# Three expert columns of a retrieval layer gathered early, without the rows of eight partitions, and those rows gathered apart

## The reference

```
def peer(h, w_query, sub_keys, expert_down, expert_up):
    # 8 heads, K = 16 experts a head: 128 experts for each of 256 tokens
    ...
    cand_id = top_i[:, :, 0, :, None] * N_KEYS + top_i[:, :, 1, None, :]
    best_s, best_c = lax.top_k(cand_s.reshape(T, PEER_HEADS, K * K), K)
    expert_id = take_along_axis(cand_id..., best_c)      # T x 128 numbers
    gate = softmax(best_s)
    ...
    u = expert_down[ib]                                  # 128 rows of 1024 for each token
    a = einsum('pd,ped->pe', xb, u)
    act = gelu(a) * gb
    v = expert_up[ib]                                    # 128 more rows of 1024
    y = einsum('pe,ped->pd', act, v)
```

## Time and profile before

| | |
|---|---|
| median of 3 runs | 1139.67 us (1138.53 to 1140.38) |
| the profiled execution | 1139.47 us, its span 1137.6 us |
| busy: PE, DVE, ACT, POOL | 1023.0, 850.4, 420.2, 288.6 us |
| DMA queue q0 (the gathers) | 37152 packets, 268.45 MB |
| mean granted TensorE clock | 0.974 |

### The profile page before, as it was taken

How to read it: one execution, slowest core, us unless ns; L and a number is a source line. 1 busy time by engine, 2 the same in 40 slices (tenths; PEclk the granted TensorE clock), 3 DMA queues, 4 the chain that set the end, 5 groups by cost and what they waited for, 6 DMA issues and landing times.

```text
span 1137.6 us, 14403 instructions
## 1 busy us (share of the span) xinstructions
PE 1023.0 (90%) x5146; PEld 711.7 (63%) x5146; DVE 850.4 (75%) x1789; ACT 420.2 (37%) x839; POOL 288.6 (25%) x262
## 2 busy tenths in 40 slices
PE   7999999999999999999999998878777778787896
PEld 7999999999998877966665554333323233333342
DVE  6988699999867984676787775776776677677555
ACT  5646544444356654352332231221221122122121
POOL 0000000000000000144455544444434435344530
PEclk9999999999999999999999999999989989898999
DMA  9533479989828334599999999999999999999995
GB/s 357 222 139 103 149 253 356 335 302 329 307 81 329 134 112 168 215 366 422 421 420 422 420 421 421 421 421 421 422 422 421 422 420 422 422 421 422 420 423 206
DMA packets 68183, 378.61 MB, mean 333 GB/s; under 512 B 7568, under 2 KB 7952, under 8 KB 35600
## 3 DMA queue, kind: packets, MB, share of 16 engines
q0 software_dynamic: 37152, 268.45, 56.9%
q1 hardware_dynamic: 29808, 106.09, 25.5%
q10 hardware_dynamic: 1152, 3.15, 0.8%
HBM read 376.61 MB, written 1.05 MB: 332 GB/s over the span
## 4 chain that ended last, share of the span: by engine, by line
PE 42%; DMA 32%; DVE 18%; ACT 4%; issue 3%; POOL 0%; SPq 0%; DVEq 0%; ACTq 0%; POOLq 0%
DMA ring_sb<-in_peer,idsb 30%; PE pb L940 8%; PE pb L943 7%; DVE ring_lo L1483 5%; PE pb L437 5%; PE pb L440 5%; PE pb L465 3%; PE pb L894 3%; DVE ring_sb L2178 2%; DVE arena L1746 2%; PE pb L819 1%; PE pb L880 1%; PE pb L655 1%; ACT whi L1003 1%; DMA arena<-in_peer,idsb 1%
## 5 line engine op out<-in xcount | busy, mean ns | idle before, releaser
L940 PE MATMUL pb<-ring_sb,arena 128*128 128x512 f32 x276 | 157.7, 655 | 79.4 <-ACT arena L1417 79.4
L2178 DVE CUSTOM_DVE_ANT_0 ring_sb<-ring_sb,arena 128x1024 f32<-128x1024 f32 x138 | 168.7, 1224 | 74.1 <-DMA ring_sb<-in_peer,idsb 72.9
L2279 POOL DMA_INDIRECT ring_sb<-in_peer,idsb x136 | 149.9, 1102 | 230.2 <-PE pb L943 205.0
L437 PE MATMUL pb<-xhi,whi 128*128 128x256 f32 x704 | 178.8, 289 | 3.6 <-DVE arena L1912 2.0
L2279 POOL DMA_INDIRECT arena<-in_peer,idsb x38 | 46.2, 1217 | 525.8 <-DVE idsb L2069 475.4
L1412 ACT ACTIVATE arena<-arena 128x4 f32<-128x4 f32 (+2 forms) x77 | 15.7, 205 | 434.0 <-DVE arena L2178 434.0
L440 PE MATMUL pb<-xlo,whi 128*128 128x256 f32 x704 | 175.7, 285 | 0.2
L1483 DVE TENSOR_TENSOR ring_lo<-ring_sb,whi 128x1024 fp32r<-128x1024 f32 x126 | 147.6, 1218 | 11.7 <-ACT whi L1003 11.7
L943 PE MATMUL pb<-ring_sb,arena 128*128 128x512 f32 x276 | 153.2, 638 | 0.0
L940 PEld LDWEIGHTS pb<-ring_sb,arena 128*128 128x128 f32 x276 | 53.4, 205 | 155.9 <-issue 155.0
L437 PEld LDWEIGHTS pb<-xhi,whi 128*128 128x128 f32 x704 | 134.6, 191 | 7.5 <-issue 3.9
(11 more groups left out here) (393 smaller groups left out, 1765.0 us busy)
## 6 DMA issues: line engine op xcount, KB each, us to landing
ring_sb<-in_ada SPq DMA_DIRECT2D x48, 512.0 KB, 5.6
ring_sb<-in_w_gu SPq DMA_DIRECT2D x44, 512.0 KB, 6.8
ring_sb<-in_w_in SPq DMA_DIRECT2D x38, 512.0 KB, 8.0
ring_sb<-in_w_down SPq DMA_DIRECT2D x22, 512.0 KB, 6.0
ring_sb<-in_w_out SPq DMA_DIRECT2D x16, 512.0 KB, 3.5
ring_sb<-in_w_q SPq DMA_DIRECT2D x8, 512.0 KB, 4.0
whi_rows<-in_w_q SPq DMA_DIRECT2D x6, 512.0 KB, 8.2
ring_sb<-in_peer,idsb POOLq DMA_INDIRECT x136, 26.8
```

Of the source, the lines that this page charges most:

```text
L437: e.matmul(o, hi_w(u)[:, c], xh(k), start=start, stop=False, skip_group_check=skip)
L940: mm = e.matmul(pb[4 + 2 * tile][:, :], dgr[col % 8], o[:, 1024:1536], start=begin, stop=end)
L2178: e.tensor_tensor_reduce(o, o, h2t[tile], 1.0, 0.0, MUL, ADD, aa[:, col:col + 1]).then_inc(*VD.up(("dot", col)))
L2279: e.indirect_dma_start(rows_at[s], None, peer, bass.IndirectOffsetOnAxis(ap=idsb[:, col:col + 1], axis=0)).then_inc(s_row[s], 16)
```

## The change

Three columns, 237 to 239, are taken out of their place in POOL's sequence. They are issued between column 219 and column 220, from a copy of the expert numbers (`kept`) in which the partitions 28 to 31 and 60 to 63 hold a number past the end of the table: DVE adds the constant `away` (16384 on these eight partitions, 0 elsewhere). The gathers have a bounds check that skips such rows. Meanwhile SP copies the real numbers of these partitions (two blocks of 4 x 3) to `apart`, on partitions 0 to 3. Right after column 233 POOL waits for these copies and for each of the three early gathers, and issues two gathers of four rows for each of the three columns, into partitions 28 to 31 and 60 to 63 of its slot. A column's semaphore now reaches its value only after all three of its gathers. The three slots aren't given back to `free`. DVE, ACT and PE work through the columns in the old order.

```diff
+    put("away", NEXP * ((p // 4 == 7) | (p // 4 == 15)))
...
+        kept, apart = sb("kept", 4, U32), sb("apart", 8, U32)
...
+        APART = range(237, 240)
+        APART_AT = (28, 60)
...
                 e.dma_start(slot(u), src).then_inc(s_slot[place[u]], 16)
+            e.wait_ge(*VTI.at(14))
+            for i, p in enumerate(APART_AT):
+                e.dma_start(apart[0:4, 4 * i:4 * i + 3], idsb[p:p + 4, APART.start:APART.stop]).then_inc(s_apart, 16)
             e.wait_ge(s_out, 64)
...
+                if n == 14:
+                    e.wait_ge(*VTI.at(n))
+                    e.tensor_scalar(kept[:, 0:3], idsb[:, APART.start:APART.stop], c_("away"), None, ADD).then_inc(*VTI.up("kept"))
...
-            for col in range(256):
+            for col in [*range(220), *APART, *range(220, 237), *range(240, 256)]:
                 s, until = free.pop(0)
-                uses[s] += 1
+                uses[s] += 3 if col in APART else 1
...
+                if col in APART:
+                    i = col - APART.start
+                    if i == 0:
+                        e.wait_ge(*VTI.at("kept"))
+                    e.indirect_dma_start(rows_at[s], None, peer, bass.IndirectOffsetOnAxis(ap=kept[:, i:i + 1], axis=0),
+                                         bounds_check=NEXP - 1, oob_is_err=False).then_inc(s_row[s], 16)
+                    continue
...
+                if col == 233:
+                    e.wait_ge(s_apart, 32)
+                    for i, c in enumerate(APART):
+                        r, v = row_of[c]
+                        e.wait_ge(s_row[r], v - 32)
+                        for j, p in enumerate(APART_AT):
+                            e.indirect_dma_start(rows_at[r][p:p + 4], None, peer,
+                                                 bass.IndirectOffsetOnAxis(ap=apart[0:4, 4 * j + i:4 * j + i + 1], axis=0)).then_inc(s_row[r], 16)
```

More of the change, by code:

```diff
@@ L41 @@
 _at = 0
-for _name, _n in (("ones", 128), ("invf", 1), ("eps", 1), ("eps2", 1), ("one", 1), ("zero", 1), ("iota", 16), ("ident", 128),
+for _name, _n in (("ones", 128), ("invf", 1), ("eps", 1), ("eps2", 1), ("one", 1), ("zero", 1), ("iota", 16), ("away", 1), ("ident", 128),
                   ("rot", 128), ("bd64", 128), ("tri", 128), ("sbm", 128), ("hgm", 128), ("fold", 32)):
@@ L205, in build @@
         s_row = [sem(f"s_row{i}") for i in range(16)]
+        s_apart = sem("s_apart")
         s_up = [sem(f"s_up{i}") for i in range(2)]
```

## The result

The changed kernel takes **1143.66 us** (median of 6 runs, 1142.78 to 1144.51), the kernel before 1139.68 (6 runs, 1138.48 to 1140.38). The ratio is 1.0037, with a 95% interval of 1.0027 to 1.0048: **slower by 0.37%, 4.0 us**, where 1133.7 was forecast. The profiled execution took 1143.42 us with a span of 1141.6, also 4.0 longer than before.

The account below looks back on a forecast made before the run. The prediction took one late DMA engine as the bound: gathers ending at 1124.1 instead of 1130.0 give -5.9 us, all other terms 0, so 1133.7 us. Its own range was 1132.3 to 1135.5; the 8-in-10 range 1131.9 to 1140.5.

Parts of the forecast that it names:

- the load of one late engine: End of the gathers: fifteen DMA engines end by 1123.6 us, one at 1130.0, 6.4 us behind, and every column waits for it.
- its windows: Sign at the end: no lone engine at 0.06 beyond a microsecond or two; share falls to 0 around 1120 to 1124.
- The waits: POOL's waits for `kept`, the early landings and SP's two copies, before column 234 at the latest: 0 us added.
- POOL's six issues: Six four-row gathers behind column 233 take POOL 7.4 us; the queue keeps 12 us of margin, so cost 0.
- the dot of column 220: Behind the three early columns, columns 220 to 236 come some 1 to 2 us later; 237 to 239 give it back.
- column 233: On POOL, column 233 takes the place of the old 236 and goes out at 1055.17 us.
- if these eight are one engine's share, and the late engine's: Eight rows skipped in three early gathers: the late engine has 7.4 us less to do and ends at 1122.6.
- The chance of 0.66: Weight of the forecast, resting on the relieved engine being the late one.
- They return by six gathers of four rows ... I take 0.5 us, the even spread: Return of 24 rows over sixteen engines: 0.5 us taken, bounds 0 to 7.4; fifteen engines then end by 1124.1.
- The first: Rival: relief misses the late engine or comes back to it, which still ends last; 1140.0 us, chance 0.17.
- The third: Rival: the queue runs dry behind column 233 while POOL issues six gathers and waits; 1144 us, chance 0.08.
- The second: Rival: relief is real, but the 24 returned rows pile up on one of the fifteen; 1138 us, chance 0.09.

Follow-up runs that it names:

- e9: Kernel before, order unchanged, columns 237 to 239 gathered without the rows of partitions 12 to 15 and 44 to 47, never brought back: 1132.95 us against 1139.04.
- e2: Kernel before with columns 237 to 239 issued early but gathered whole, no four-row gathers or SP copies: 1138.76 us against 1139.15.
- e3: Changed kernel without the six four-row gathers and SP's copies, the skipped rows of 28/60 left out for good: 1138.89 us against 1139.15.
- e6: Kernel before, order unchanged, sixteen columns each gathered without the eight rows of a different partition set: 1136.92 us against 1139.3.
- e12: Kernel before plus six four-row gathers after column 236 into unused arena, four to 28/60, two to 92/124: 1142.96 us, ratio 1.0034.
- e14: e12 with all row numbers past the end of the table, so no data moves: 1138.97 us against 1139.14.
- e5: e3 with POOL held before column 234 until PE has used column 226: 1139.53 us against 1139.3.
- e13: e12 with each gather's four rows placed eight partitions apart: 1141.55 us, ratio 1.0020.
- e18: e12 with four gathers (16 rows), all to partitions 12 to 15 and 44 to 47: 1144.59 us, ratio 1.0049.
- e15: Kernel before plus six gathers of sixteen rows after column 236, on partitions 16 to 31, 64 to 79 and 80 to 95: 1146.85 us, ratio 1.0067.
- e17: e12 with four gathers (16 rows), all to partitions 28 to 31 and 60 to 63: 1142.43 us against 1138.98.
- e10: Changed kernel with partitions 12 to 15 and 44 to 47 in place of 28/60, nothing left out: 1140.29 us, ratio 1.0012.
- e16: Changed kernel at 12/44, one four-row gather after each of columns 228 to 233, nothing left out: 1139.42 us, ratio 1.0003.

## Why the prediction was wrong

**What held.** The bound is the load of one late engine: e9 gained 6.1 us where 5.9 to 6.4 was worked out, and its windows look as the prediction drew them. The waits cost nothing as costed: the move and `kept` by e2 and e3, SP's copies by what is left over (the whole change +4.0, the six gathers alone +3.9). POOL's six issues took 7.7 us, for 7.4. In before's kernel and this one alike one engine ends last, alone. Two times on the way were off and cost nothing: the dot of column 220 comes 7.3 us later than in before (1050.23 against 1042.94), not 1 to 2, and column 233 goes out at 1064.60, not at 1055.17; `e2` has the same gap and loses nothing.

**First step that failed: "if these eight are one engine's share, and the late engine's".** The first half held (e6, e9: one set of eight rows is one engine's, 2.5 us). The second did not: 24 rows off 28/60 saved 0.0 (e3). The chance of 0.66 rested on "by judgement and without a row", and the text itself said that fifteen of sixteen are others. The Trainium skill (DMA: Bandwidth & Descriptors, section The descriptor swizzle) gives 12/44 to engine 3, 28/60 to engine 7 and 92/124 to engine 15, and its section Latency and other measured facts calls 7 and 15 the usually slower ones. The runs agree on the set of 12/44 as one engine's share, but skipping the rows that the page gives to 7 or 15 gained nothing, and those of 3 gained 6.1 us; the measurement decides. What made the engine late here, q14's packets, the prediction didn't look for.

**Second step that failed: "They return by six gathers of four rows ... I take 0.5 us, the even spread".** It cost 3.9 us (e12). The upper bound written there, 7.4, held; the value was taken from the nearest rows, all of which show 128-row gathers. And it was added to the wrong place: as load on fifteen engines that had 6.4 us to spare. The late engine lost it too, +2.8 us at column 231 and +1.05 at column 234.

What the runs show of this term: no cost without data (e14), none from dry queues (e5), the whole of it without any moved row (e12), less with spread rows (e13: 2.4), more to the late engine's own partitions (e18: 5.6 for two thirds of the rows). What is shown is that the packets of the gathers beside them are stretched (e12). An account that fits most of it, and is argued: while a small gather is worked off, its rows queue up at one target, and the other engines wait for it. Then a gather costs its rows per set x 0.31 us. e15 has 16 rows over four sets, 4 x 0.31 = 1.24 us, x 6 = 7.4; measured 7.7. e13: one row per set, 6 x 0.31 = 1.9; measured 2.4. e18: 4 x 1.24 = 5.0; measured 5.6. e12 would be 7.4 and is 3.9; e17 would be 5.0 and is 3.4. `e15` reaches the full sum though none of its sets is the late engine's. So for four rows in one set it is an upper bound, and why these cost 0.5 to 0.7 of it is **open**: the fifteen have slack of 6.4 us, but no run separates how much of the hold-up the late engine escapes. This sum was made after the runs, and no run tested it. The Trainium skill (DMA: Bandwidth & Descriptors, section Back-pressure in remote DMA) says that a saturated destination SBUF port clogs the path back to the source engines and to engines that share it. It says so of transfers between cores; full shares at 90 to 266 GB/s agree with it on one core, but no row here shows a port.

**The rivals.** The first (relief misses, 1140.0) had the mechanism half right and lacked the price of the return. The third named the place and nearly the time (1144), but not the mechanism: POOL was late there and queues may have run dry, yet e5 shows that this costs nothing as long as the late engine has work. A right number was no evidence for its cause. The second (24 rows pile up) is the nearest in mechanism; it counted the pile on one engine with slack, where several are held up.

**Why the right partitions don't help either.** With the rows of 12/44 left out the time is 6.1 us lower (e9); with the same rows brought back it is 1.3 higher (e10). The return thus costs 7.3 us there (1140.29 - 1132.95), as much as the 24 x 0.31 = 7.4 taken off. Brought singly and early (e16) it is 6.4 us. The other engines pay too: in e10 the last but one landing of column 253 is 5.3 us later than in before, so that little of their slack is left. That the rows pay on arrival just what they saved, whoever brings them, is suggested by these numbers and by e18, and not shown. No version with all its work done beat the kernel before; 1132.95 only shows what the late engine costs.

## What to carry to other kernels

When every column waits for one late DMA engine, first find which partitions are its own by skipping one set of rows at a time (one run, e6), before moving work on a guess, and look in the trace for what else the engine carries. Here rows taken out of a full-width gather and brought back by small gathers to the same partitions cost all that they had saved, so price a new kind of transfer by an added-only kernel (e12) rather than by the even spread of the full ones. A gap of 10 us on PE or POOL isn't a loss when a transfer queue is the bound, and a low rate is to be read with its share: in these traces a low share meant no work, and a full share at a low rate meant stretched packets.

## What was not expected of the hardware

- Gathers of few rows slow all the traffic beside them: 421 GB/s fell to 90 to 266 for 6 us (after), 168 to 230 for 4 us (e12). Per row 0.16 us in blocks of four (e12; 0.22 in e17), 0.10 spread (e13), 0.08 in sixteens (e15: 7.7 / 96), 0.35 to the late engine's partitions (e18).
- A four-row gather leaves 12 small packets and takes 0.87 to 1.26 us of POOL, as a 128-row one does; with no row in range it costs the traffic nothing (e14).
- The late engine is the one that writes partitions 12 to 15 and 44 to 47. It is late, not slow: one 8 KB packet of q14 costs it about 0.97 us while its queue is full, and eight of them between 632 and 1114 us come to 7.8 us. No run was made with fewer such packets.
